# Rotary exchange in the attention stage split between ScalarE and VectorE, its steps in another order, and one score step of the recurrent stage set two slots later

## What is computed

```python
def apply_rope(x, cos, sin):
    x1, x2 = jnp.split(xf, 2, axis=-1)
    return jnp.concatenate([x1 * cos - x2 * sin, x2 * cos + x1 * sin], axis=-1)

def mla(...):
    q = (rms_norm(c_q, g_cq) @ w_uq).reshape(B, L, MLA_HEADS, QK_NOPE_DIM + QK_ROPE_DIM)   # 128 + 64
    q_nope, q_rope = q[..., :QK_NOPE_DIM], q[..., QK_NOPE_DIM:]
    q_rope = apply_rope(q_rope, cos, sin)
    ...
    s = (q_nope @ k_nope.T + q_rope @ k_rope.T) * scale      # per head
    o = softmax(s) @ v

def gla_chunkwise(q, k, v, g):     # CHUNK = 64, forward and backward
    ...
    a = where(causal, einsum(q_r, k_r), 0)                   # scores inside a chunk
    o = a @ v_c + (q_c * exp(b)) @ S
    S = exp(b_last) * S + (k_c * exp(b_last - b)).T @ v_c
```

## Time and profile before

| | |
|---|---|
| median of 3 runs | 2129.88 us (2128.2 to 2131.61) |
| profiled execution, its own time | 2132.09 us |
| its span, first to last instruction | 2130.1 us |
| TensorE busy | 2059.7 us, 97% |
| VectorE, ScalarE, GpSimd busy | 1273.3, 950.5 and 439.0 us |
| mean granted TensorE clock | 0.994 of full speed |

### The profile page before, as it was taken

How to read it: one execution, slowest core, us unless ns; L and a number is a source line. 1 busy time by engine, 2 the same in 40 slices (tenths; PEclk the granted TensorE clock), 3 DMA queues, 4 the chain that set the end, 5 groups by cost and what they waited for, 6 DMA issues and landing times. The chain is left out here.

```text
span 2130.1 us, 32695 instructions
## 1 busy us (share of the span) xinstructions
PE 2059.7 (97%) x12456; PEld 1738.6 (82%) x12456; DVE 1273.3 (60%) x1934; ACT 950.5 (45%) x1558; POOL 439.0 (21%) x273
## 2 busy tenths in 40 slices
PE   8999999999999999979999999999999999999999
PEld 8998888788888888768888887777888888888886
DVE  3403665855856658457787788468766667652532
ACT  6314454453644554545555555455433233343422
POOL 1110000000000000132222221120254545424443
PEclk9999999999999999989999999999999999999999
DMA  5111122121121120321111110444322222344452
GB/s 189 63 55 60 46 65 62 41 66 59 49 62 41 64 70 26 115 86 42 44 43 44 41 44 25 157 174 144 134 80 75 84 84 94 138 164 158 152 187 89
DMA packets 79391, 182.11 MB, mean 85 GB/s; under 512 B 7008, under 2 KB 27808, under 8 KB 77632
## 3 DMA queue, kind: packets, MB, share of 16 engines
q1 hardware_dynamic: 79296, 180.82, 25.0%
HBM read 142.39 MB, written 38.40 MB: 85 GB/s over the span
## 5 line engine op out<-in xcount | busy, mean ns | idle before, releaser
L88 PE MATMUL h_bank<-hn_hi,w_hi 128*128 128x512 f32 (+2 forms) x952 | 369.4, 388 | 2.8 <-ACT raw L716 1.6
L90 PE MATMUL h_bank<-hn_hi,w_lo 128*128 128x512 f32 (+2 forms) x952 | 353.1, 371 | 0.0
L89 PE MATMUL h_bank<-hn_lo,w_hi 128*128 128x512 f32 (+2 forms) x952 | 352.7, 371 | 0.0
L88 PEld LDWEIGHTS h_bank<-hn_hi,w_hi 128*128 128x128 f32 x952 | 179.0, 188 | 33.0 <-issue 8.7
L90 PEld LDWEIGHTS h_bank<-hn_hi,w_lo 128*128 128x128 f32 x952 | 178.7, 188 | 27.8
L89 PEld LDWEIGHTS h_bank<-hn_lo,w_hi 128*128 128x128 f32 x952 | 179.1, 188 | 26.8 <-issue 3.8
L716 ACT COPY raw<-h_bank 128x512 f32<-128x512 f32 (+2 forms) x119 | 63.9, 543 | 273.5 <-PE h_bank L90 243.1
L2256 ACT CAST w_hi<-w_raw 128x1024 fp32r<-128x1024 f32 x79 | 82.8, 1050 | 216.9 <-PE f_bank L90 208.9
L1136 POOL MEMSET ckv_hi<- 128x224 f32 x1 | 0.3, 285 | 744.9 <-POOLq L584 744.9
L889 DVE TENSOR_TENSOR w_lo<-w_raw,w_hi 128x1024 fp32r<-128x1024 f32 x52 | 63.5, 1221 | 147.7 <-ACT w_hi L696 147.7
L2226 POOL TENSOR_TENSOR w_lo<-w_raw,w_hi 128x1024 fp32r<-128x1024 f32 x45 | 108.4, 2408 | 144.9 <-ACT w_hi L2256 144.9
(11 more groups left out here) (431 smaller groups left out, 5305.4 us busy)
## 6 DMA issues: line engine op xcount, KB each, us to landing
w_raw<-in_w_ffn SPq DMA_DIRECT2D x82, 512.0 KB, 3.5
w_raw<-in_w_hgrn SPq DMA_DIRECT2D x54, 512.0 KB, 3.4
raw_up<-in_w_ffn SPq DMA_DIRECT2D x18, 512.0 KB, 4.7
hidden<-gate_blocks SPq DMA_DIRECT2D x34, 256.0 KB, 2.0
w_raw<-in_w_out SPq DMA_DIRECT2D x15, 512.0 KB, 4.4
X<-in_x SPq DMA_DIRECT2D x8, 520.0 KB, 9.1
values<-values_h SPq DMA_DIRECT2D x32, 128.0 KB, 1.7
values_h<-values SPq DMA_DIRECT2D x8, 512.0 KB, 4.6
```

The lines of the kernel that those rows point to most:

```text
L88: pe.matmul(out, wh, xh, start=start, stop=False)
L89: pe.matmul(out, wh, xl, start=False, stop=False)
L90: return pe.matmul(out, wl, xh, start=False, stop=stop)
```

## The change

Three things are changed.

1. The exchange of quarters goes to ScalarE as four plain copies of 32 rows (two after `high` of block 0, two after that of block 1), and the product with the sine becomes one instruction of VectorE on 128 rows, ahead of `rope_add`. The sign pattern of the sine table is turned, since it now applies after the exchange. GpSimd has no rotary work left.
2. The order of the rotary steps is another. In a segment, `rope_high` goes from block 1 (both) to blocks 2 and 3 (one each), and `rope_low` from block 2 to the end of the segment (first half) or to the next head's first segment, after its pieces 1 and 3 (second half). In `begin`, `rope_high` no longer stands behind the cast of the values, which goes to block 1; the second half's projection goes from block 2 to block 0, and piece 4 from block 3 to block 2. A score block now waits only for the low part of its own head of the pair.
3. In the recurrent stage `inside` 0 goes from slot 56 to 58 and `updates` 4 from 58 to 60.

```diff
-            (43, "turn", 3), (45, "turn", 4), (47, "updates", 2), (53, "updates", 3), (56, "inside", 0),
-            (58, "updates", 4), (67, "outputs", 0), (75, "norm_sum", 0), (77, "inside", 1), (83, "outputs", 1),
+            (43, "turn", 3), (45, "turn", 4), (47, "updates", 2), (53, "updates", 3), (58, "inside", 0),
+            (60, "updates", 4), (67, "outputs", 0), (75, "norm_sum", 0), (77, "inside", 1), (83, "outputs", 1),
...
# GpSimd
-                def swap(p, half):
-                    rope_raw.wait(pool, pair(p), half + 1)
-                    rope_added.wait(pool, pair(p), half)
-                    for to, rows in enumerate(SWAPS):
-                        src = SWAPS[to ^ 1]
-                        rope_swapped.wait(pool, pair(p), 4 * half + to)
-                        pool.tensor_tensor(q_swapped[rows, :], q_raw[src, :],
-                                           turn_table[1][src, half * HALF:(half + 1) * HALF], ALU.mult
-                                           ).then_inc(rope_swapped.sem, 1)
...
# ScalarE
+                def swap(p, half, n):
+                    rope_added.wait(act, pair(p), half)
+                    for to in (2 * n, 2 * n + 1):
+                        act.copy(q_swapped[SWAPS[to], :], q_raw[SWAPS[to ^ 1], :]).then_inc(rope_swapped.sem, 1)
...
                             high(cur, 2 * j + 2)
+                            if j < 2 and even(p):
+                                swap(p, which, j)
+                            if j > 1 and even(p):
+                                rope_high(p, which, j - 2)
                             if 2 * j + 3 < TILES:
                                 high(cur, 2 * j + 3)
...
-                        if j == 1 and even(p):
-                            rope_high(p, which)
...
                 def begin(p):
                     raw_rope(p, 0)
+                    for n in range(2):
+                        swap(p, 0, n)
                     for i in range(NP_ - 1):
                         piece(p, i)
-                    values(p)
-                    rope_high(p, 0)
+                    rope_high(p, 0, 0)
+                    rope_high(p, 0, 1)
+                    raw_rope(p, 1)
                     for j in range(QS):
                         softmax((p, 0), j)
                         if j == 1:
-                            raw_rope(p, 1)
+                            values(p)
                         if j == 2:
                             piece(p, NP_ - 1)
                             weights(p, 2)
-                    rope_high(p, 1)
+                    for n in range(2):
+                        swap(p, 1, n)
+                    rope_high(p, 1, 0)
+                    rope_high(p, 1, 1)
...
# VectorE
                     rope_swapped.wait(dve, pair(p), 4 * (half + 1))
+                    dve.tensor_tensor(q_swapped, q_swapped, turn_table[1][:, half * HALF:(half + 1) * HALF],
+                                      ALU.mult).then_inc(rope_sin.sem, 1)
+                    rope_sin.wait(dve, pair(p), half + 1)
...
+                            if i == 1 and not even(p) and not begins(cur[0]):
+                                rope_low(cur[0], 1, 0)
                     if even(p):
                         rope_by_cos(p, which)
+                    elif p is not None and which == 0 and not begins(cur[0]):
+                        rope_low(cur[0], 1, 1)
...
-                        if even(p) and j == 2:
-                            rope_low(p, which)
...
+                        if even(p) and which == 0:
+                            rope_low(p, 0, 0)
+                            rope_low(p, 0, 1)
...
# VectorE, begin: rope_by_cos(p, 1) ahead of the blocks instead of in block 1
# TensorE
-                        rope_lo.wait(pe, pair(x), 2 * i + 2)
+                        rope_lo.wait(pe, pair(x), 2 * i + x.base % 2 + 1)
...
                     for j in range(QS):
+                        if j == 0:
+                            project_rope(p, 1)
                         if j == 2:
-                            project_rope(p, 1)
-                        if j == 3:
                             project(p, NP_ - 1)
...
-    a["turns"] = np.stack([np.concatenate([cos] * 4), np.concatenate([sin, -sin] * 2)])
+    a["turns"] = np.stack([np.concatenate([cos] * 4), np.concatenate([-sin, sin] * 2)])
```

More of the change, by code:

```diff
@@ L1440, in both @@
                     for which, (cur, nxt) in enumerate(segments(p, h)):
[L1441 to L1446, removed]
                         if p is not None:
@@ L1489, in raw_rope, with rope_high @@
                     act.copy(q_raw[:], rope_bank(p, half)).then_inc(rope_raw.sem, 1)
-                def rope_high(p, half):
+                    rope_raw.wait(act, pair(p), half + 1)
+                def swap(p, half, n):
+                    rope_added.wait(act, pair(p), half)
+                    for to in (2 * n, 2 * n + 1):
+                        act.copy(q_swapped[SWAPS[to], :], q_raw[SWAPS[to ^ 1], :]).then_inc(rope_swapped.sem, 1)
+                def rope_high(p, half, b):
                     rope_added.wait(act, pair(p), half + 1)
-                    for b in range(2):
-                        s_done.wait(act, p, (half + 1) * QS, lag=2 - b)
-                        act.copy(q_rope[b, half][ROWS[b], :], q_turned[ROWS[b], :]).then_inc(rope_hi.sem, 1)
+                    s_done.wait(act, p, (half + 1) * QS, lag=2 - b)
+                    act.copy(q_rope[b, half][ROWS[b], :], q_turned[ROWS[b], :]).then_inc(rope_hi.sem, 1)
                 def values(p):
@@ L1605, in rope_add, with rope_low @@
                     rope_swapped.wait(dve, pair(p), 4 * (half + 1))
+                    dve.tensor_tensor(q_swapped, q_swapped, turn_table[1][:, half * HALF:(half + 1) * HALF],
+                                      ALU.mult).then_inc(rope_sin.sem, 1)
+                    rope_sin.wait(dve, pair(p), half + 1)
                     rope_cos.wait(dve, pair(p), half + 1)
                     dve.tensor_tensor(q_turned[:], q_turned[:], q_swapped, ALU.add).then_inc(rope_added.sem, 1)
-                def rope_low(p, half):
-                    for b in range(2):
-                        rope_hi.wait(dve, pair(p), 2 * half + b + 1)
-                        dve.tensor_tensor(q_rope[b, half][ROWS[1 - b], :], q_turned[ROWS[b], :],
-                                          q_rope[b, half][ROWS[b], :].bitcast(F32), ALU.subtract
-                                          ).then_inc(rope_lo.sem, 1)
+                def rope_low(p, half, b):
+                    rope_hi.wait(dve, pair(p), 2 * half + b + 1)
+                    dve.tensor_tensor(q_rope[b, half][ROWS[1 - b], :], q_turned[ROWS[b], :],
+                                      q_rope[b, half][ROWS[b], :].bitcast(F32), ALU.subtract
+                                      ).then_inc(rope_lo.sem, 1)
                 def find_top(nxt, j):
@@ L1707, in begin @@
                     rope_add(p, 0)
-                    rope_low(p, 0)
+                    rope_low(p, 0, 0)
+                    rope_low(p, 0, 1)
+                    rope_by_cos(p, 1)
                     for j in range(QS):
@@ L1713, in begin @@
                             normalize((p, 0), j - 1)
-                        if j == 1:
-                            rope_by_cos(p, 1)
                         if j == 2:
@@ L1719, in begin @@
                     rope_add(p, 1)
-                    rope_low(p, 1)
+                    rope_low(p, 1, 0)
+                    rope_low(p, 1, 1)
                 def both(p, h):
```

3 lines of the change are left out of this document (1 added, 2 removed).

## The result

| | before | after |
|---|---|---|
| median | 2129.92 us (2128.2 to 2131.61, 4 runs) | 2116.01 us (2113.99 to 2117.33, 4 runs) |
| profiled execution, its own time | 2132.09 us | 2113.99 us |
| its span | 2130.1 us | 2112.2 us |

The ratio is 0.9932, with a 95% interval of 0.9916 to 0.9948: the change makes the kernel faster, by 13.9 us. The forecast was 22.5 us, and 2116.0 lies above the high end of the range (2114).

What follows compares the result with a forecast made beforehand. TensorE, busy 97% of the span, was taken as the bound, so only its pauses could be won: 8.5 (recurrent) + 10.5 (loop) + 3.5 (begin) = 22.5 us, giving 2107.4 us from the median; range 2102 to 2114.

Steps and rivals of the forecast that it cites:

- the loop's term: Attention loop, six segments with an even p: TensorE's pauses go, 10.5 us gained, bounds 6 and 11.
- the sine product costs its bare time: Loop, block 1: VectorE's added product takes about 0.6 us, with GpSimd taken as idle there.
- the subtractions of the first half: Loop: moved into about 2 us in which VectorE waits at the segment's change, so hidden.
- The removal of the two subtractions: Loop, even segments: 1.33 us of VectorE less ahead of the last low part, which then ends at 1022.85.
- GpSimd's exchange "undisturbed": Loop: without GpSimd's four products the first two low parts come 0.7 us earlier, covering waits of 0.15 and 0.32.
- Copies hidden: Loop, blocks 0 and 1: two ScalarE copies of 0.62 us each fit its waiting time; second cast 0.1 us late, hidden.
- Rival A: Even segments: ScalarE late with copies of 0.9 us or more, or last low part still late; 2113 us, chance 0.14.
- Recurrent, 8.5 forecast: Recurrent stage: 1.15 us gained in each of 6 heads, about 0.8 in the other two; bounds 6 and 9.4 us.
- The wait on scores: Recurrent stage, `outputs` 0: TensorE comes earlier and newly waits 0.2 us for the scores.
- Rival B: Recurrent stage: scores replace factors as the wait, their chain starting 0.3 to 0.7 us later; 2112 us, chance 0.09.
- begin, 3.5 forecast: `begin`: second key piece of head 1 starts 4.5 us earlier, less 1 us for the clock; bounds 0 and 6.
- My 1 us for half clock: `begin`: taken off the 4.5 us gain, since 3 us of half speed behind the last pause would cost 1.5.

Runs made afterwards that it cites:

- e3: The changed kernel with the exchange and the sine product back on GpSimd, everything else in the new order; 2109.61 us, ratio 0.9904 to the kernel before.
- e4: The changed kernel with GpSimd's values, weights and mixed sum held in the loop until VectorE's rotary steps are through; 2113.86 us, ratio 0.9923 to before.
- e5: The changed kernel with `outputs` 0 of the recurrent stage at slot 68 instead of 67, nothing else; 2113.82 us, ratio 0.9924 to before.
- the change's second profile: The changed kernel run again with no edit; median 2114.19 us, ratio 0.9924 to the kernel before.
- e9: The kernel before with the exchange alone moved to ScalarE and VectorE, every other step where it stood; 2143.38 us, ratio 1.0061 to before.

## Why the prediction was wrong

The step that failed is a sentence of the loop's term: "the sine product costs its bare time wherever GpSimd is idle, as it now is at block 1". GpSimd isn't idle there. I took its exchange away and forgot its three other products, though the weights' w_lo stood in the earlier trace rows and the prediction itself quoted 2.75 us beside v_lo. The same sentence's product did cost 0.69; it pushed the *sum* under the weights, where it took 1.94 us. In e3, without the product, the sum starts at 1028.06 and the weights at 1028.48. A second step failed beside it: the subtractions of the first half, moved to the segment's change, were to fall into waiting time there, but the second of them met the mixed sum and took 1.67 us instead of 0.69. This one is the smaller: e3 has it too, and TensorE waits only 0.19 us there for the query piece behind it.

- *Loop, 10.5 us forecast, 6.9 measured.* The removal of the two subtractions and the first low parts were sized right in sum: e3 gives 10.5. What was missing is a loss of 1.13 us a pair (e4) by the meetings at 1018.00 and 1031.90.
- *GpSimd's exchange "undisturbed"* was credited as a gain for the first low parts. L1597 did fall to 0.68 us, but e3, which keeps the exchange on GpSimd, waits only 0.2 us a pair for a first low part.
- *Copies hidden:* right, 0.617 us each; e4 shows that they cost nothing in the loop. Rival A named the sign of the error, for causes that the rows exclude: copies of 0.9 us, or a last low part that stays late, for which TensorE waits just once, 0.2 us.
- *Recurrent, 8.5 forecast, 7.3 measured.* The wait on scores came as computed. Mis-sized by 0.22 us a head: 0.13 inside `outputs` 0, which e5 gives back, and 0.07 since the way from the same projection to `inside` 0 now takes two slots and 0.32 us (1.69) and took 1.62. Rival B's later chain didn't come: the scores end 8.55 us after `inside` 0 starts, before 8.53.
- *begin, 3.5 forecast, 2.4 measured.* Each wait came within 0.4 us of its forecast, yet the fourth exponential ended 29.5 us after the start, not 27.7. Of these 1.8 us, 0.3 lie ahead of the rotary terms of block 0 (12.34 us after the start, forecast 12.07) and 0.4 in the waits of 1.19 and 1.45 us (forecast 1.1 each, and up to 0.8 more for v_lo on VectorE's block 2). The other 1.1 is a sum that the prediction gave without its terms: from those rotary terms to the exponential's end it left 15.65 us (925.45 to 941.1), and the rows after, with waits of 1.1 us, make 16.75. My 1 us for half clock wasn't needed in this execution and hid half of the error; in the change's second profile, 1.6 us of this kind did come, in the pass behind `begin`.
- *Profile against median.* I took 2.2 us off for a slow profiled execution. The change's own profiled execution was 2.0 us faster than its first median. Summed with the true terms (7.3 + 2.4 + 6.9 - 0.7 = 15.9 from 2132.09) the chain gives 2116.2 for the profiled execution and 2114 for the median, between the two medians measured (2116.01 and 2114.19).

What the move of the exchange costs `begin` can be read from two traces: to the second key piece of head 1 e3 takes 34.94 us and the change 36.28, and 1.21 of these 1.34 us are there already at the rotary terms of block 0 (11.13 against 12.34 us after the start), ahead of which the change has four copies and a wait of 1.20 us. Open is how far e9's 13.9 us are the edit's: its stages explain 9 (three pairs 6.5, `begin` 2.5). Its profiled execution is 12.6 us longer than that of before, and the rest lies in half-speed stretches or where the edit changes nothing: a later pair of 106.35 us beside the 104.75 of the table, with rows of TensorE of 0.63 us where others have 0.39 (1.6), the pass behind `begin` at a granted clock of 0.95 (48.82 us, before 46.79), and 1.5 us ahead of the recurrent stage.

At this place the Trainium skill, SBUF — State Buffer, section "Summary: rules for kernel authors", says that of a VectorE instruction with two SBUF inputs and a GpSimd instruction that reads SBUF the second to issue is fully blocked until the first has finished. The rows where VectorE came second agree: the sum, 0.24 us behind the weights, ended 0.54 us after them, the subtraction at 1018.00 ended 0.55 us after the mixed sum, and the one-column shift of 2.26 us ended at 930.30, v_lo at 930.28. The Trainium skill, SBUF — State Buffer, section "Who interferes with whom", says that a VectorE instruction with at most one SBUF input, outside the 2-port modes, doesn't contend with GpSimd, and the low part of the probabilities, which reads PSUM and one SBUF tile, kept 0.68 us beside v_lo (1008.50). The rule for GpSimd's exchange was in the prediction; it was not applied to GpSimd's other products.

## What to carry to other kernels

When work leaves an engine, list what else that engine does at the new places of the moved steps before pricing them: a two-input product on VectorE costs its row's time plus whatever is left of the GpSimd instruction that it meets. Price the parts of a composite change apart, since a gain from order can hide a loss from placement, here 20 us against 5. And where two kernels differ by a few us in 2100, compare the lengths of stages and the periods of loops in the traces, where the granted clock is the same in both; the medians move by 2 us for reasons of their own.

## What was unexpected

- A VectorE instruction on 128x1 elements took 2.26 us beside GpSimd's v_lo and 0.22 alone, and it stood on the chain of shift, exponential and bank, so TensorE paid for it. The kernel before shows this too: in its `begin` the same instruction takes 1.01 us at 940.40, beside the exchange.
- VectorE's normalisation, 128x1040 with a single tensor input, took 1.57 us beside GpSimd's exchange in e3 (at 928.07; before, 1.60 at 941.71) against 0.76 alone, so the meeting is not confined to products of two tensors.
- A wait of 0.23 us showed in the trace as a distance of 0.46 us between two starts where 0.23 is usual, with no idle time named.
